# Attention by pairs of heads, with the keys and values projected first and the query chunks in between

## What is computed

```
x  = rmsnorm(x, g_final)                 # end of the first block
hn = rmsnorm(x, norm_mix[0])             # start of the second
q, k, v = split(hn @ w_qkv)              # 1024, 256 and 256 columns
q, k = axial_rope(rmsnorm(q, q_g)), axial_rope(rmsnorm(k, k_g))    # per head of 64
p  = softmax(q @ k.T / 8)                # 256 x 256 per head; four query heads share a key head
x  = x + (p @ v) @ w_o
x  = x + square(relu(rmsnorm(x, norm_mlp[0]) @ w_in)) @ w_out
```

## Time and profile before

| | |
|---|---|
| time, three runs | 1036.0, 1037.59 (median), 1040.18 us |
| the profiled execution | 1035.37 us, its span 1033.6 us |
| first matmul of the first `qkv` chunk | at 392.0 us of the span |
| first matmul of `wo` | at 497.3 us |
| mean granted clock of TensorE | 0.972 of full speed |

### The profile page before, as it was taken

One profiled execution on the slowest core, in us unless ns is written; L12 is line 12 of the kernel. 1 busy time (PEld: TensorE's weight loads), 2 busy tenths in 40 slices (PEclk: granted clock), 3 DMA queues, 4 the chain that ended last, 5 costly groups with the idle time before them and its releaser, 6 DMA issues.

```text
span 1033.6 us, 18040 instructions
## 1 busy us (share of the span) xinstructions
PE 949.0 (92%) x7517; PEld 894.1 (87%) x7517; DVE 663.3 (64%) x1035; ACT 507.7 (49%) x719; POOL 2.9 (0%) x6
## 2 busy tenths in 40 slices
PE   5599899889999998979999999997988799999997
PEld 2487777789999997955889999997988789999997
DVE  0754464676767679876585665666885866665564
ACT  3535963545555557446553434435665544434432
POOL 1000000000000000000000000000000000000000
PEclk9799999989999999989999999999999899999999
DMA  9976566455455554310347456544532346456531
GB/s 348 325 239 219 163 235 239 152 180 205 164 204 167 201 189 137 124 51 1 123 132 254 167 178 214 181 147 159 163 123 82 122 133 226 173 172 210 189 123 41
DMA packets 122284, 177.15 MB, mean 171 GB/s; under 512 B 3088, under 2 KB 103996, under 8 KB 122076
## 3 DMA queue, kind: packets, MB, share of 16 engines
q1 hardware_dynamic: 121260, 173.97, 49.7%
q10 hardware_dynamic: 944, 2.03, 0.6%
HBM read 174.68 MB, written 1.05 MB: 170 GB/s over the span
## 4 chain that ended last, share of the span: by engine, by line
PE 72%; DVE 14%; ACT 6%; DMA 5%; issue 3%; SPq 0%; DVEq 0%; ACTq 0%
PE psum L1439 21%; PE psum L1440 21%; PE psum L1441 21%; DVE w_lo L834 3%; DMA raw<-in_w_in_dram 2%; DMA raw<-in_w_ada_dram 2%; PE psum L1727 1%; PE psum L1526 1%; ACT w_hi L485 1%; PE psum L1707 1%; DVE work L873 1%; DMA raw<-in_w_out_dram 1%; ACT h_hi L496 1%; PE psum L1542 1%; PE psum L1771 1%
## 5 line engine op out<-in xcount | busy, mean ns | idle before, releaser
L1439 PE MATMUL psum<-h_hi,w_hi 128*128 128x256 f32 x1384 | 397.0, 287 | 42.1 <-DVE w_lo L834 16.2
L1440 PE MATMUL psum<-h_lo,w_hi 128*128 128x256 f32 x1384 | 392.6, 284 | 0.0
L1441 PE MATMUL psum<-h_hi,w_lo 128*128 128x256 f32 x1384 | 392.3, 283 | 0.0
L485 ACT ACTIVATE w_hi<-raw 128x2048 fp32r<-128x2048 f32 (+1 forms) x139 | 264.7, 1905 | 153.1 <-PE psum L1441 103.6
L834 DVE TENSOR_TENSOR w_lo<-raw,w_hi 128x2048 fp32r<-128x2048 f32 (+1 forms) x139 | 313.0, 2275 | 2.7 <-ACT w_hi L485 2.6
L1439 PEld LDWEIGHTS psum<-h_hi,w_hi 128*128 128x128 f32 x1384 | 267.0, 193 | 51.2 <-issue 32.6
L1440 PEld LDWEIGHTS psum<-h_lo,w_hi 128*128 128x128 f32 x1384 | 267.3, 193 | 0.1
L1441 PEld LDWEIGHTS psum<-h_hi,w_lo 128*128 128x128 f32 x1384 | 267.0, 193 | 0.0
L1439 PE MATMUL psum<-a_hi,w_hi 128*128 128x256 f32 x688 | 192.1, 279 | 0.3 <-DVE w_lo L834 0.2
L1441 PE MATMUL psum<-a_hi,w_lo 128*128 128x256 f32 x688 | 191.8, 279 | 0.0
L1440 PE MATMUL psum<-a_lo,w_hi 128*128 128x256 f32 x688 | 191.8, 279 | 0.0
(11 more groups left out here) (263 smaller groups left out, 870.6 us busy)
## 6 DMA issues: line engine op xcount, KB each, us to landing
raw<-in_mlp_w_in_dram SPq DMA_DIRECT2D x32, 1024.0 KB, 5.4
raw<-in_mlp_w_out_dram SPq DMA_DIRECT2D x32, 1024.0 KB, 6.6
raw<-in_w_ada_dram SPq DMA_DIRECT2D x24, 1024.0 KB, 7.0
raw<-in_w_up_dram SPq DMA_DIRECT2D x22, 1024.0 KB, 5.1
raw<-in_gla_w_in_dram SPq DMA_DIRECT2D x12, 1024.0 KB, 5.6
raw<-in_w_down_dram SPq DMA_DIRECT2D x11, 1024.0 KB, 5.4
raw<-in_w_in_dram SPq DMA_DIRECT2D x10, 1024.0 KB, 7.6
raw<-in_attn_w_qkv_dram SPq DMA_DIRECT2D x6, 1024.0 KB, 5.3
```

What stands on the lines that cost most here:

```text
L485: act.activation(halved(w_hi, m % SPLIT_SLOTS, SPLITS[m]), halved(raw, r % RAW_SLOTS, SPLITS[m]), ACT.Copy).then_inc(*mark("w_hi", m))
L1439: pe.matmul(dst, lhs[0], rhs[0], start=start, stop=False, skip_group_check=True)
L1440: pe.matmul(dst, lhs[0], rhs[1], start=False, stop=False, skip_group_check=True)
L1441: return pe.matmul(dst, lhs[1], rhs[0], start=False, stop=stop, skip_group_check=True)
```

## The change

It has these parts. Keys and values are projected first, queries after them, half a chunk at a time, with attention steps in between. Attention goes by pairs of heads: the two heads of a pair take the upper and lower 64 partitions of one query tile `aq` and of the turned keys `ak`; the zeros, the doubled keys and their DMAs are gone. For that the query chunks are loaded with their columns in another order, in four parts of 64 columns per chunk, and the rows of `w_o` likewise, in four parts of 64 partitions. Both norms' sums come from one pass over `x_t` (squares of `x_t` and of `x_t` times `g_final`), roots are made as exp(-ln/2) on ScalarE under one table, and `x_t` is rescaled only when `wo` is added. The low split of the second `qkv` chunk stands ahead of `add_down`. From pair 2 on, the result is split straight from its bank.

```diff
-QKV = [0, 1, 2, 4, 5, 3]
+K_CHUNK, V_CHUNK = 0, 1
+EARLY = 2
...
+    s += [("add_down", "down"), ("unscaled", 3)] + [("squares", 2, n) for n in range(4)] + [("squares", 3, n) for n in range(4)]
+    s += [("tree", 2), ("tree", 3), ("qkv", 0), ("qkv", 1, 0), ("sums",), ("qkv", 1, 1), ("k_a", 0), ("k_a", 1),
+          ("qkv", 2, 0), ("r_cols", 3), ("k_b", 0), ("k_b", 1), ("q_a", 0), ("values",), ("qkv", 2, 1), ("q_a", 1),
+          ("k_c", 0), ("q_b", 0), ("q_b", 1), ("q_scale", 0), ("k_c", 1), ("qkv", 3, 0), ("att_a", 0), ("q_a", 2),
+          ("qkv", 3, 1), ("q_a", 3), ("att_a", 1), ("q_b", 2), ("q_b", 3), ("q_scale", 1), ("att_scale", 0),
+          ("qkv", 4, 0), ("att_b", 0), ("att_a", 2), ("q_a", 4), ("att_scale", 1), ("qkv", 4, 1), ("att_o", 0),
+          ("att_y", 0), ("att_b", 1), ("q_a", 5), ("att_a", 3), ("q_b", 4), ("q_b", 5), ("q_scale", 2), ("att_scale", 2),
+          ("qkv", 5, 0), ("att_o", 1), ("att_y", 1), ("att_b", 2), ("q_a", 6), ("att_a", 4), ("att_scale", 3),
+          ("qkv", 5, 1), ("q_a", 7), ("att_o", 2), ("att_b", 3), ("split", 4, 0), ("split", 4, 1), ("att_y", 2), ("att_a", 5), ("q_b", 6), ("q_b", 7),
+          ("q_scale", 3), ("att_scale", 4), ("att_o", 3), ("att_b", 4), ("att_y", 3), ("att_a", 6), ("att_scale", 5),
+          ("att_o", 4), ("att_b", 5), ("att_y", 4), ("att_a", 7), ("att_scale", 6), ("att_o", 5), ("att_b", 6), ("att_y", 5),
+          ("att_scale", 7), ("att_o", 6), ("att_b", 7), ("att_y", 6), ("att_o", 7), ("att_y", 7)]
...
+        aq, ak, v2 = area(6, 8), area(14, 2), area(16, 2)
+        att_p = area(22, 8).rearrange("p (b q) s -> p b q s", b=4)
+        att_pt = area(30, 8).rearrange("p (b q) s -> p b q s", b=4)
...
+                    c0 = 2 * S * ((n - 2) // 2) + P * ((n - 2) % 2)
+                    return [(P * j + HD * e, column_chunk(w, c0 + S * e + HD * j, HD)) for j in range(2) for e in range(2)], KT
...
+            def sums():
+                act.wait_ge(*at("job", "sum", 2))
+                act.activation(rstd[:, :], bank("sum", 2)[:, 0:S], ACT.Ln, scale=1.0 / D, bias=cst("eps"))\
...
+                act.activation(spare[:, 0, :], rstd[:, :], ACT.Exp, scale=-1.0).then_inc(*mark("first_squared", 0))
...
+                act.activation(rstd_x[:, :], spare[:, 1, :], ACT.Exp, scale=-0.5).then_inc(*mark("rstd_both", 3))
...
-                act.preload_act_table_set("sqrt_and_others")
+                act.preload_act_table_set("natural_log_exp_and_others" if key[0] == "down" else "sqrt_and_others")
...
-                        .then_inc(*mark(f"k_doubled{2 * t + n}", 0, by=16))
...
-                ahead(key)
+                ahead(key, 2 if key == ("down", FF_STEPS - 1) else 1)
...
+                        if kind == "wo":
+                            dve.scalar_tensor_tensor(out=x_t[:, k, :], in0=x_t[:, k, :], scalar=col("g_final", k),
+                                                     in1=rstd[:, :], op0=ALU.mult, op1=ALU.mult).then_inc(*mark("x_new", 3, k))
+                            dve.wait_ge(*at("x_new", 3, k))
...
-                    dve.memset(aqz, 0.0).then_inc(*mark("gain_qkv", 0))
...
+            def att_scale(t):
+                dve.wait_ge(*at("act_read", "att", t, 1))
+                dve.reciprocal(pair_small(t, 3), pair_small(t, 2)).then_inc(*mark("att_rden", t))
...
+            def att_a(t):
+                pe.wait_ge(*at("turn", t))
+                pe.wait_ge(*at("k_turned", t // 4))
+                dst = [take(pe, "att", t, n) for n in range(2)]
+                for n in range(2):
+                    half = slice(HD * n, HD * n + HD)
+                    for q in range(TT):
+                        ins = pe.matmul(dst[n][:, q * S:(q + 1) * S], aq[half, t, q * P:q * P + P], ak[half, t // 4, :],
+                                        start=True, stop=True, skip_group_check=True)
+                ins.then_inc(*mark("job", "att", t))
...
+            def att_o(t):
+                pe.wait_ge(*at("act_read", "att_t", t, 1))
+                pe.wait_ge(*at("act_read", "qkv", V_CHUNK, 1))
+                dst = take(pe, "att_o", t)
+                for n in range(2):
+                    g = 2 * (t // 4) + n
                     for k in range(TT):
...
+                        ins = pe.matmul(dst[HD * n:HD * n + HD, 0:S], v2[:, k, g * HD:g * HD + HD],
+                                        att_pt[:, 2 * (t % 2) + n, k, :], start=(k == 0), stop=(k == TT - 1),
+                                        skip_group_check=True)
+                ins.then_inc(*mark("job", "att_o", t))
```

More of the change, by code:

```diff
@@ L358, in build, with pair_small @@
         y_rows = raw[:, 0:2, 0:D]
+        def pair_small(t, first):
+            o = 16 * (t % 2) + 4 * first
+            return small[:, o:o + 4]
         def wview(buf, slot, kt):
@@ new lines, in values, with q_scale @@
+            def values():
+                for m in range(TT):
+                    act.wait_ge(*at("dve_read", "r_cols", 3))
+                    copy(("qkv", V_CHUNK, m), v2[:, m, :], ACT.Identity, scale=r_col[:, m:m + 1])
+            def q_scale(c):
+                act.wait_ge(*at("q_mean", 2 * c + 1, 1))
+                f = q_mean[:, :, 4 * c:4 * c + 4]
+                act.activation(f, f, ACT.Ln).then_inc(*mark("q_log", c))
+                act.wait_ge(*at("q_log", c))
+                act.activation(f, f, ACT.Exp, scale=-0.5).then_inc(*mark("q_factor", c))
@@ L1662, in add_down, with qkv, sums @@
                 ring["set"] = range(8)
-            def qkv(n):
-                project_chunk(3, ("qkv", n), token_tile if n == 4 else feature_tile)
+            def qkv(n, m=None):
+                if m is None:
+                    project_chunk(3, ("qkv", n))
+                    return
+                (token_tile if n == V_CHUNK else feature_tile)(3, ("qkv", n), m)
+                if m == 1:
+                    used(("qkv", n), ("job", "qkv", n, 1))
+            def sums():
+                dst = take(pe, "sum", 2)
+                for i, src in ((2, work), (3, squares_g)):
+                    pe.wait_ge(*at("tree", i, 2))
+                    ins = pe.matmul(dst[:, (i - 2) * S:(i - 1) * S], cst("ones"), src[:, 0, :], start=True, stop=True,
+                                    skip_group_check=True)
+                ins.then_inc(*mark("job", "sum", 2))
             def total(i):
@@ L1692, in k_b @@
                 pe.wait_ge(*at("k_square", t))
[L1693 removed]
+                pe.matmul(take(pe, "k_mean", t)[:, 0:S], cst("head_mean"), k_sq[:, t, :], start=True, stop=True)\
                     .then_inc(*mark("job", "k_mean", t))
@@ new lines, in att_b @@
+            def att_b(t):
+                for n in range(2):
+                    pe.wait_ge(*at("att_scaled", t, n, 1))
+                    dst = take(pe, "att_t", t, n)
+                    for q in range(TT):
+                        for k in range(TT):
+                            ins = pe.transpose(dst[:, k * S + q * P:k * S + q * P + P],
+                                               att_p[:, 2 * (t % 2) + n, q, k * P:k * P + P], cst("ident"))
+                    ins.then_inc(*mark("job", "att_t", t, n))
```

308 lines of the change are left out of this document (140 added, 168 removed).

## The result

The changed kernel took 1013.6 us in the median of three runs (1010.7 to 1015.2) against 1037.8 for the kernel before: a ratio of 0.9758, with a 95% interval of 0.9727 to 0.9788. Another comparison gave 1013.3 against 1035.8, 0.9773 (0.9748 to 0.9799). 1018 was predicted, a gain of 18.3 us; 22 to 24 came. The profiled execution took 1012.11 us.

What follows compares the result with a forecast made beforehand. TensorE, busy for 92%, was taken to bound the kernel by its work, waits and slow clock. -12.6 (attention stage), -6.2 (memset) and +0.5 (rescaling) gave -18.3, so 1018 us; range about 1006 to 1031.

Steps and rivals of the forecast that it cites:

- rival B: Attention: score matmuls of row halves overlap, gaining 3.5 us between projections and 1 in the tail: 1013.5 us; chance 0.12.
- A: The main forecast for the whole kernel: 1018 us; chance 0.53.
- part 3: Attention woven between projections, walked in order: `qkv` to `wo` 91.3 us, VectorE's loop bounding the tail; -12.6 us.
- Part 1: Pairs of heads on array halves: 5.0 us of TensorE per pair, no gain from halves at once; pairing 0.2 us.
- Part 2: Start of the attention stage: with the low split ahead of `add_down`, the first `qkv` matmul comes 1.4 us later.
- Part 4: First MLP: without VectorE's memset, TensorE's 4.02 us wait and the low clock after it go; -6.2 us.
- Part 5: Rescaling of `x_t` moved behind `wo`: only the last tile's is on the path, +0.5 us; table load 0.
- Part 6: Query chunks loaded in 256-byte pieces: 6.3 us a chunk, cost 0 to 2 us, taken as 0.
- C: Query loads late at 50 ns a 256-byte piece, ScalarE 8 us late: 1026 us; chance 0.09.
- E: Slower: query loads at 60 ns a piece lose most of the 18 us, at 70 ns 1040 to 1045; chance 0.05.
- D: Attention stalls on semaphore hops or the clock falling to half: 8 us more, 1026 us; chance 0.14.
- F: Little gain: a tail of 7 us periods, another wait in the memset's place: 1034 to 1038 us; chance 0.07.

Runs made afterwards that it cites:

- scores_ahead: Changed kernel with TensorE's scores of pairs 6 and 7 one step earlier, their maxima and exponentials ahead of `att_y`: 1008.9 us, 0.9741 to the kernel before.
- after_again: The changed kernel itself, unedited, measured once more: 1013.3 us, 0.9773 to the kernel before; stage 86.4 us.

## Why the prediction was right, and where not

**What the runs bear out is rival B.** The forecast, A, was 1018 and B 1013.5; 1013.3 to 1013.6 came, all within the range. The overlap of the halves, B's mechanism, is shown, and at 0.12 of the chances it was under-rated. That 1018 came within 5 us is partly luck, as part 3 shows: a large error in TensorE's work and three in the other direction nearly cancelled.

**Part 1** failed, on scores and values. "The scores of both halves are issued in the order A A B B, so all but one step of them is in line" was an argument without a row, and the earlier trace rows stood against it, though less clearly than rival B read it: its 4.6 at once is more than the four quarters there are, since records of MATMUL overlap without tiles too (in the kernel before, those of `wo` last 0.28 us and start 0.12 apart, 2.4 at once). The order A A B B turned out to be no hindrance (the order A B A B was not tried). The Trainium skill (TensorEngine Tiling (Array Packing), Key Properties) says that different tiles can load and multiply in parallel. The runs agree: the eight loads take 0.74 us on two halves and 1.59 on one. The values' 1.76 us was a row misread. In the earlier trace rows the second head waited for its copy on ScalarE; this row of the kernel before belongs beside it (ScalarE's timeline):

```profile
495.61 0.60 ACT L721 ACTIVATE arena<-psum 128x512 f32<-128x512 f32 x1 [2.61 <-PE psum L1716]
```

It ends at 496.2, the second head's four loads of 0.62 come after it, and that makes 496.8; the group ends at 496.9. A group of eight with a wait inside looks like eight in a row. Pair: 3.1 us, not 5.0.

**Part 2**: +1.4 forecast, +1.0 measured.

**Part 3**: 91.3 us forecast, 86.2 to 88.1 measured. TensorE's work is 15 us under the forecast, the stage only 3 to 5, because three things went the other way (the mean stage is 4.4 under the forecast). "TensorE waits for about 1 us only" missed the 2.27 us behind pair 0's exponentials. "The clock I take as full" was wrong: 0.93 over 47.4 us, 0.80 over 28.2. And the tail couldn't use the time. Its period was forecast at 5.5 to 5.9 us as VectorE's loop and is 5.4, but that agreement is luck. The walk's loop had TensorE's scores at 2.1 us in it, which take 1.1 and aren't in the ring at all; in their place the ring has 3.6 us of ScalarE, of which the forecast said that it "isn't the bound", and both engines stand idle for 2 us. The walk's name for the bound would have sent one to shorten VectorE's work, where moving one step past another (`scores_ahead`) gained. Chunk 5 ends 59.3 us after the stage's start, 60.6 forecast.

Rival B's own sum gave the tail 1 us and the weave 3.5, of overlapping scores alone: stage 86.8, in the middle of what was measured. That too is partly luck, for the values overlap as well, and the waits and the clock named above took that back. Taking either overlap away costs more than B's 4.5 by the mean stage (5.0 and 6.6), with more lost to the clock in both runs than in `after_again`; how much is the overlap's own at equal clock stays open.

**Part 4**: -6.2 forecast, -6.5 between the two traces, 5.5 when put back alone. The split ran where it was said to, with full clock.

**Part 5**: +0.5 forecast for the last rescale; the wait at `wo`'s end grew by 0.25, and from the first `wo` to the first `gla` matmul `after_again` takes 24.4 against 23.9. Not forecast: in the first profile, whose tail ends at a clock of 0.65, `wo` begins below full clock, and the same way takes 25.3.

**Part 6** and rivals C and E: 4.8 us a chunk against 6.3 taken, cost 0. The Trainium skill (DMA: Bandwidth & Descriptors, Specifications) wants at least 512 bytes for line rate. The rate agrees below that, 218 GB/s for 256 bytes, but 512-byte pieces at 330 are already under the 380 of 1 KB pieces. Nothing came late for it, and whether small pieces are read, modified and written no run here shows. Rivals D and F: D's low clock was there, its loss outweighed by what B gained; F's period of 7 us and its other wait did not occur.

## What to carry over

Ask of two small products whether they sit on different rows or columns of the array, and test whether they run at once before pricing them one after the other; here a pair of heads on halves cost TensorE the time of one in scores and in value products. Before a group's duration is used as a price, look at the other engines inside it for a wait. In a tail, write down the ring through all engines' lists in order: if no engine is full in its period, look for a wait that can move behind independent work. And compare a tail by itself, not only the whole stage: a single execution's clock ahead of it can hide what an edit did in it.

## What the runs showed of the hardware

- 64-row halves loaded in the order A A B B overlap: eight loads in 0.74 us, 1.59 on one half; 64-column halves 0.64 against 1.49.
- Single executions of kernels alike in their first 200 us differ there by up to 8.6 us (197.87 to 206.42 at the same split), and the later ones show a lower granted clock between 30 and 130 us. Medians differ too, 1008.9 and 1012.8 us for `scores_ahead`; that this has the same cause was not shown.
- A clock brought to full by useless work (0.83 and 0.65 to 1.00) left the ring's period at 5.43 us and made the tail about 1 us shorter.
- 256-byte pieces: 218 GB/s, 18.8 ns each per engine; 512-byte pieces 330 GB/s, 1 KB pieces about 380.
